# A routed-expert decoder layer on one core: a reworked routing stretch, reordered first transfers, an attention bias added on VectorE, earlier expert loads, and filler matmuls

## The reference, cut to what matters

```python
h = rms_norm(x, norm1_g);  z = h @ w_in            # 11,272 columns
qk = silu(causal_dwconv(concat(qm, km), conv_w))
hm = sigmoid(om) * head_layernorm(mlstm(...));  ha = attention(..., rel_bias)
y = sigmoid(gm) * (hm @ w_branch_m) + sigmoid(ga) * (ha @ w_branch_a)
x = x + y @ w_out
t = rms_norm(x, norm2_g)
pg = softmax(t @ w_grp + b_grp);  el = t @ w_exp + b_exp      # 4 groups, 32 experts
# best group, its best two experts, weights pg * pe / sum(pe)
x = x + sum_e combine[:, e] * ((silu(t @ w1[e]) * (t @ w3[e])) @ w2[e])
out = rms_norm(x, final_g)
```

## Time and profile before

| what | value |
|---|---|
| median of 3 runs | 1272.96 us (1272.76 to 1274.13) |
| the profiled execution: its own time, its span | 1268.82 us, 1267.3 us |
| TensorE matmul busy, weight load busy | 1183.3 us (93%), 886.9 us (70%) |
| DVE, ACT, POOL busy | 689.1 us, 413.2 us, 44.9 us |
| mean granted TensorE clock | 0.986 of full speed |
| expert weight loads | 96 into `w_a` and 96 into `w_b`, 1024 KB each |
| DMA, 40 slices | 130 to 250 GB/s up to the output projection, 425 GB/s in nearly all slices of the experts |

### The profile page before, as it was taken

The page is one execution under the profiler, slowest core; times in us unless marked ns, Lnnn a source line. Parts: engine busy times, 40 slices in busy tenths (PEclk is TensorE's granted clock), DMA queues, the critical chain, the costliest instruction groups (busy, mean ns, idle before and its releaser), DMA issues.

```text
span 1267.3 us, 19180 instructions
## 1 busy us (share of the span) xinstructions
PE 1183.3 (93%) x7194; PEld 886.9 (70%) x7194; DVE 689.1 (54%) x980; ACT 413.2 (33%) x463; POOL 44.9 (4%) x57
## 2 busy tenths in 40 slices
PE   5999999999999999999999985899999999899995
PEld 4888888888888888888888875555554544444442
DVE  4678555554666657567875547243444433433335
ACT  4444333334334354443344443111111211111113
POOL 1000000001002022000000002000000000000000
PEclk9999999999999999999999987999999999999998
DMA  7765565655555455555765635899999999999993
GB/s 245 226 190 175 166 193 172 195 174 178 185 165 167 134 164 165 165 166 182 251 177 181 236 148 226 342 402 425 426 426 425 425 425 425 425 425 424 425 425 150
DMA packets 170146, 336.52 MB, mean 266 GB/s; under 512 B 12144, under 2 KB 136192, under 8 KB 153088
## 3 DMA queue, kind: packets, MB, share of 16 engines
q1 hardware_dynamic: 163088, 335.58, 71.8%
q10 hardware_dynamic: 7024, 0.48, 0.4%
HBM read 333.93 MB, written 2.11 MB: 265 GB/s over the span
## 4 chain that ended last, share of the span: by engine, by line
PE 56%; issue 39%; ACT 1%; DVE 1%; ACTq 1%; POOL 1%; POOLq 0%; DVEq 0%
PE ps L824 19%; PE ps L840 11%; PE ps L826 10%; PE ps L842 6%; PE ps L973 5%; PE ps L974 2%; PE ps L813 1%; POOL h2lo L552 1%; PE ps L942 0%; PE ps L993 0%; ACTq L564 0%; DVE wsplit L1149 0%; ACT xsq L572 0%; ACT h2n L744 0%; ACT wsplit L581 0%
## 5 line engine op out<-in xcount | busy, mean ns | idle before, releaser
L1149 DVE TENSOR_TENSOR wsplit<-wraw,wsplit 128x2048 fp32r<-128x2048 f32 x120 | 277.1, 2309 | 180.5 <-ACT wsplit L581 179.7
L824 PE MATMUL ps<-act_split,wsplit 128*128 128x512 f32 x1024 | 360.7, 397 | 0.0
L581 ACT ACTIVATE wsplit<-wraw 128x2048 fp32r<-128x2048 f32 x120 | 230.0, 1917 | 386.7 <-PE ps L826 204.7
L826 PE MATMUL ps<-act_split,wsplit 128*128 128x256 f32 x1024 | 286.6, 280 | 0.0
L840 PE MATMUL ps<-wsplit,act_split 128*128 128x512 f32 x640 | 226.8, 398 | 2.1 <-DVE wsplit L1149 2.1
L824 PEld LDWEIGHTS ps<-act_split,wsplit 128*128 128x128 f32 x1024 | 192.0, 188 | 46.1 <-DVE wsplit L1149 1.3
L826 PEld LDWEIGHTS ps<-act_split,wsplit 128*128 128x128 f32 x1024 | 193.3, 189 | 0.2
L842 PE MATMUL ps<-wsplit,act_split 128*128 128x256 f32 x640 | 179.2, 280 | 0.0
L840 PEld LDWEIGHTS ps<-wsplit,act_split 128*128 128x128 f32 x640 | 120.1, 188 | 31.3 <-issue 2.7
L1056 PE MATMUL ps<-w_a,xe 128*64 128x256 f32 x1024 | 115.4, 381 | 13.8 <-DMA w_a<-in_w_dram 12.0
L1595 DVE TENSOR_TENSOR hid<-sg,ps 128x128 f32<-128x128 f32 x32 | 9.2, 288 | 206.0 <-ACT sg L769 206.0
(11 more groups left out here) (274 smaller groups left out, 1082.0 us busy)
## 6 DMA issues: line engine op xcount, KB each, us to landing
w_a<-in_w_dram SPq DMA_DIRECT2D x96, 1024.0 KB, 19.0
w_b<-in_w_dram SPq DMA_DIRECT2D x96, 1024.0 KB, 21.3
wraw<-in_w_in_dram SPq DMA_DIRECT2D x88, 1024.0 KB, 5.1
wraw<-in_w_out_dram SPq DMA_DIRECT2D x16, 1024.0 KB, 5.1
wraw<-in_w_branch_m_dram SPq DMA_DIRECT2D x8, 1024.0 KB, 5.1
wraw<-in_w_branch_a_dram SPq DMA_DIRECT2D x8, 1024.0 KB, 5.1
xin<-in_x_dram SPq DMA_DIRECT2D x2, 1024.0 KB, 6.5
x<-in_x_dram SPq DMA_DIRECT2D x1, 2048.0 KB, 9.3
```

What stands on the lines that cost most here:

```text
L581: act.activation(wsplit[:, q % 2, :, 0], wraw[:, q % RAW], ACT.Copy).then_inc(rounded, 1)
L824: pe.matmul(banks[b], w[:, k, 0, b * P:(b + 1) * P], a, start=first and k == 0, stop=False)
L826: last = pe.matmul(banks[b][:, 0:T], w[:, k, 1, b * P:(b + 1) * P], a[:, 0], start=False, stop=last_half and k == HALF_K - 1)
L1149: dve.tensor_tensor(wsplit[:, q % 2, :, 1], wraw[:, q % RAW], wsplit[:, q % 2, :, 0].bitcast(F32), ALU.subtract).then_inc(split, 1)
```

## The change

- *Start.* SP no longer waits between x and the first four weight loads. Five of the nine parameter DMAs move from ACT's queue to SP's, behind these four loads, with a semaphore of their own (`late_loaded`). POOL makes the identity first (`ident_ready`); TensorE runs 12 filler matmuls of it and then transposes the four early parameter rows. DVE squares the second token tile. The product of `relb` and `onehot_s`, the split of `wif` and the trip of the bias through DRAM come after the first units.
- *Bias.* `flip` and its matmuls are gone; DVE adds the bias to the logits (read and written with reversed columns) into `prob`, and ACT takes the exponential from there.
- *Output projection.* ACT also rounds x2 (without the norm) to `x2hi`, DVE subtracts (`x2lo`) unit by unit. The router sums accumulate in two PSUM regions over all units. The last unit is multiplied in three passes of 256 columns in place of 512 and 256, so that no sum of halves is needed, and DVE squares it.
- *Routing.* The norm is left out of the gather; an extra gather of `rms_rep` gives `slot_rms`, by which DVE multiplies when it makes `xe`. The second mask `mk[:, :, 1]` becomes a running sum along the experts (`tensor_tensor_scan`). TensorE runs 20 filler matmuls after the router sums and 12 after the rank sums. POOL no longer works on `h2lo`.
- *Loads.* The hidden weights of expert 1, `w2_b0` and `w2_b1` are loaded as each ring slot comes free in the last halves; `w2_a1` waits for `x2lo_ready`, and `w2_a0` for the gather.

```diff
 sync:
             for t in range(TT):
                 sp.dma_start(xin[:, t], x_v[:, t]).then_inc(x_loaded[t], 16)
-            sp.wait_ge(par_loaded, 16 * 9)
...
             pair(COL_QK, None)
+            sp.dma_start(wif_raw[:], ...).then_inc(late_loaded, 16)
+            sp.dma_start(ifb[:], if_bias.partition_broadcast(P)).then_inc(late_loaded, 16)
+            sp.dma_start(relb[:], rel_bias).then_inc(late_loaded, 16)
+            sp.dma_start(onehot_s[:], onehot).then_inc(late_loaded, 16)
+            sp.dma_start(g2T[:], ...).then_inc(late_loaded, 16)
+            pairs(1, UNITS_QK, COL_QK, 0)
             sp.wait_ge(rev_ready, 1)
             sp.dma_start(rev_dram, rev[:]).then_inc(rev_stored, 16)
             sp.wait_ge(rev_stored, 16)
...
-            pairs(1, UNITS_QK, COL_QK, 0)
...
             for kh in range(2):
                 load_hidden(0, 0, kh)
+            for kh in range(2):
+                sp.wait_ge(split, HALVES + 2 * kh - 2)
+                load_hidden(1, 1, kh)
+            sp.wait_ge(used, HALVES - 1)
+            load_rows(0, lambda b: b, (1,))
             sp.wait_ge(used, HALVES)
-            for kh in range(2):
-                load_hidden(1, 1, kh)
-            load_rows(0, lambda b: b)
+            load_rows(1, lambda b: b + 2, (1,))
             sp.wait_ge(routed, 1)
+            sp.wait_ge(x2lo_ready, UNITS_OUT)
             load_rows(1, lambda b: b + 2, (0,))
-            sp.wait_ge(xg_summed, DC)
-            load_rows(1, lambda b: b + 2, (1,))
+            sp.wait_ge(xg_summed, DC + 1)
+            load_rows(0, lambda b: b, (0,))
 gpsimd:
-            for t, cols in ((0, slice(0, D)), (1, slice(0, D // 2))):
-                pool.wait_ge(h2hi_ready, t + 1)
-                pool.tensor_tensor(h2lo[:, t, cols], h2n[:, t, cols], h2hi[:, t, cols].bitcast(F32),
-                                   ALU.subtract).then_inc(h2lo_ready, 1)
 tensor:
+            for n in range(WARM):                                   # 12
+                pe.matmul(ps[:, 6, 0:P], ident[:], ident[:], start=True, stop=True)
...
-                    pe.matmul(bank[:, 0:P], flip[:], bias[:, 0, P:T], start=False, stop=True)
...
-                    pe.matmul(bank[:, P:REV], flip[:], bias[:, 0], start=False, stop=True).then_inc(logits, 1)
...
+            def token_half_in_place(banks, q, first, last_half):
...
+                        pe.matmul(banks[t][:, 0:UNIT], hi, w[:, k, 0], start=first and k == 0, stop=False)
+                        pe.matmul(banks[t][:, 0:UNIT], hi, w[:, k, 1], start=False, stop=False)
+                        last = pe.matmul(banks[t][:, 0:UNIT], lo, w[:, k, 0], start=False, ...)
...
+            out_pair(UNITS_OUT // 2 - 1, end=True)
+            route(UNITS_OUT // 2 - 1, 0)
             turn_x2(1, UNITS_OUT - 1)
+            route(UNITS_OUT // 2 - 1, 1).then_inc(routed, 1)
+            for n in range(WARM_ROUTE):                             # 20
+                pe.matmul(ps[:, 6, 0:P], ident[:], ident[:], start=True, stop=True)
...
+            for n in range(WARM_SELECT):                            # 12
+                pe.matmul(ps[:, 6, 0:P], ident[:], ident[:], start=True, stop=True)
...
+                    if c is None:
+                        last = pe.matmul(ps[:, n % 8], rms_rep[:, t], sel[:, t].bitcast(F32), ...)
 vector:
+            steps.done(dve.scalar_tensor_tensor(xsq[:, 1], xin[:, 1], 1.0, xin[:, 1], ALU.mult, ALU.mult,
+                                                accum_out=stat[:, 1:2]))
...
+                    dve.tensor_tensor(prob[:, a, P - 1::-1], ps[:, 4 + a, P - 1::-1], bias[:, 0:P], ALU.add)
+                    steps.done(dve.tensor_tensor(prob[:, a, REV - 1:P - 1:-1], ps[:, 4 + a, REV - 1:P - 1:-1],
+                                                 bias[:, 0:T], ALU.add))
...
+            def x2_split(n, u, start):
+                dve.wait_ge(x2hi_ready, n + 1)
+                cols = ds(start, UNIT)
+                dve.tensor_tensor(x2lo[:, :, cols], x2u[:, u], x2hi[:, :, cols].bitcast(F32),
+                                  ALU.subtract).then_inc(x2lo_ready, 1)
...
-            unit_sums = ...
-            for u in range(2):
-                last = dve.tensor_reduce(unit_sums[:, u]..., ps[:, 2 + u, ...]..., AX.X, ALU.add)
+            for t in range(TT):
+                last = dve.scalar_tensor_tensor(lr[:, t], ps[:, 2 + t, 0:n_r], stat[:, 22 + t:23 + t], brt[:],
+                                                ALU.mult, ALU.add)
...
-            dve.tensor_tensor(rt[:, 3], iota_t, by_token(FIRST, EXPERTS), ALU.is_gt)
...
-            steps.done(dve.tensor_tensor(rt[:, 1], iota_t, by_token(FIRST, EXPERTS), ALU.is_gt))
-            dve.tensor_tensor(mk[:, :, 1], rt[:, 3], rt[:, 1], ALU.add).then_inc(mk_ready, 1)
+            x2_split(UNITS_OUT - 1, 1, D - UNIT)
+            for t in range(TT):
+                dve.tensor_scalar(rms_rep[:, t], ones[:], stat[:, 22 + t:23 + t], None, ALU.mult)
...
-                    dve.tensor_copy(xe[:, b], xg[:, :, ds(at, SLOTS)]).then_inc(xe_ready, 1)
+                    factors = slot_rms[:, ds(at, SLOTS)].unsqueeze(1).to_broadcast([P, DC, SLOTS])
+                    dve.tensor_tensor(xe[:, b], xg[:, :, ds(at, SLOTS)], factors, ALU.mult).then_inc(xe_ready, 1)
```

More of the change, by code:

```diff
@@ L623, in _ @@
             conv_pair(0)
+            act.wait_ge(late_loaded, 16 * 5)
+            act.activation(wif[:, :, 0], wif_raw[:], ACT.Copy).then_inc(wif_hi, 1)
             with act.Fori(1, UNITS_QK // 2 - 1) as i:
@@ L724, in out_unit @@
                 act.wait_ge(x2_ready, n + 2)
-                act.activation(x2[:, :, ds(i * (2 * UNIT) + u * UNIT, UNIT)], x2u[:, u], ACT.Copy)
+                if end and u == 1:
+                    x2T_copy(u, n)
+                act.activation(x2[:, :, cols], x2u[:, u], ACT.Copy)
+                act.activation(x2hi[:, :, cols], x2u[:, u], ACT.Copy).then_inc(x2hi_ready, 1)
+                if end and u == 1:
+                    return
                 if not first_unit(i, u):
@@ L865, in _ @@
                 half(channel_half, q, q, None)
+            pe.wait_ge(consts, 1)
+            pe.wait_ge(late_loaded, 16 * 5)
+            pe.matmul(ps[0:A_HEADS, 6, 0:T], relb[:], onehot_s[:], start=True, stop=True).then_inc(rev_summed, 1)
             stage(channel_half, 0, 1, UNITS_QK)
@@ L1032, in _ @@
             last.then_inc(rank_summed, 1)
+            for n in range(WARM_SELECT):
+                pe.matmul(ps[:, 6, 0:P], ident[:], ident[:], start=True, stop=True)
             pe.wait_ge(sel_ready, 1)
[L1036 to L1044 removed]
+            pe.wait_ge(x2lo_ready, UNITS_OUT)
@@ new lines, in _ @@
+            parts = [part[:].rearrange("p t (q c) -> p t c q", c=DC) for part in (x2hi, x2lo)]
+            for n, c in enumerate(gathers):
+                if n >= 8:
+                    pe.wait_ge((xg_act, xg_dve)[n % 2], (n - 8) // 2 + 1)
+                for t in range(TT):
+                    if c is None:
+                        last = pe.matmul(ps[:, n % 8], rms_rep[:, t], sel[:, t].bitcast(F32), start=t == 0, stop=t == TT - 1)
+                        continue
+                    for k, part in enumerate(parts):
+                        last = pe.matmul(ps[:, n % 8], part[:, t, c], sel[:, t], start=t == 0 and k == 0,
+                                         stop=t == TT - 1 and k == 1)
@@ L1302, in _ @@
             dve.wait_ge(o_ready, 1)
-            with steps.loop(0, M_HEADS, 9) as i:
+            dve.wait_ge(flip_loaded, 16 * A_HEADS)
+            with steps.loop(0, M_HEADS, 11) as i:
                 def ahead(q):
```

217 lines of the change are left out of this document (111 added, 106 removed).

## The result

The changed kernel takes 1257.51 us, the median of four runs (1255.45 to 1259.09). The kernel before, in four runs beside it, takes 1272.86 (1268.77 to 1274.13). The ratio is 0.9881, with a 95% interval of 0.986 to 0.9902: faster by 15.3 us. I had forecast 1255.5 within 1250.5 to 1261.5.

What follows compares the result with a forecast made beforehand. TensorE's passes bound the dense stages, the weight stream the experts. Terms -4.6 + 0.4 - 5.3 - 8.0 = -17.5 from the profiled 1268.8 gave 1251.3, plus 4.1 to the median: 1255.5 us, range 1250.5 to 1261.5.

Steps and rivals of the forecast that it cites:

- The bound: From the first expert's upper half on, the weight stream sets the time; using that half earlier moves the end equally.
- Start: Launch to first dense pass: 4.6 us less, with bounds of 5.5 and 3.
- DVE squares tile 2 when it lands: At the start, DVE's square was to run from 8.3 to 9.1 for some 2.4 us, with L813 at 12.5.
- lower bound (3): At the start, only 3 us gained if the weight loads right behind x hold the parameters up.
- Relative bias: In the dense stages, the `relb` product moves into TensorE's full time, two passes of 256 columns: +0.4 us.
- Bias: In the dense stages, TensorE saves 0.66 us for each of 8 heads: -5.3 us; DVE's additions fit its idle time.
- Last halves: Output projection, three passes of 256 columns instead of 512 and 256: taken as 0, bounds 0 and +3.3 us.
- Routing: From the last dense pass to the first expert: -8.0 us in sum.
- POOL's collision: In routing, DVE's two-SBUF-input instructions L1521 and L1486 are slowed beside POOL's L552; without POOL's work -6.0 us.
- a clock of 1.00 through both fillers: Expected sign in the changed profile: TensorE at full clock during the 20 and the 12 routing fillers.
- rival 1: Routing fillers at half clock stand in the way: +4 us at the first gap, +1 at the second, 1260 to 1262; chance 0.12.
- the other reading: Unbroken routing fillers lift the clock themselves, so not all 40 passes are slow: price 1 to 2 us rather than 4.

Runs made afterwards that it cites:

- a_sq_first: The changed kernel with DVE's square of the second token tile put ahead of the parameter copy: 1256.93 us, 0.9881 of before.
- b_lo_on_dve: The kernel before with POOL's part of `h2lo` moved to DVE, behind the mask: 1269.08 us, 0.9978 of before.
- b_dve_bias: The kernel before with the bias alone changed, added by DVE without flipped-identity matmuls: 1266.54 us, 0.9962 of before.
- b_copy: The kernel before, unchanged, profiled again: 1273.59 us, 1.0012 of before.

## Why the prediction was right, and where its terms were off

**The bound.** From the load that the first expert releases to the end, 470.15 us before and 470.33 after. What comes earlier there is gained in full, and the later pairs hide DVE's multiply of `xe`. In the eleven other traces it is 469.3 to 471.0. What the earlier expert loads are worth no run shows alone; the forecast gave them nothing, and the sum leaves nothing for them.

**Start: -3.4, not -4.6.** The step that failed is "DVE squares tile 2 when it lands". It waited for the parameters, at 9.08. My lower bound (3) named the weight loads holding up the parameters; the size is nearly that, but no run shows that the loads are what held them up. a_sq_first puts 0.9 us on the order of DVE's program: there the square starts at 8.69, when x lands, and L819 at 12.65, near my 12.5. "I give them nothing" of the start's fillers was wrong too: without them the first dense pass is 0.6 to 1.7 us later. And I took the diagonal product's 8.6 us as fixed: it took 8.78 to 9.61 us in four executions of the same start, 10.16 without fillers, and 7.31 and 7.38 with ten more.

**Relative bias: +2.0, not +0.4.** The product costs 0.7 where I had 0.4; the other 1.3 are the slower pace of the halves behind it, which other executions of before have too (b_lo_on_dve), so it may be chance and not the change. The trip through DRAM is hidden, as forecast: TensorE's only wait over 0.7 us in 22 to 750 is the 2.1 us behind DVE's `wsplit`, which before has as well.

**Bias: -5.3, confirmed** by the four iterations and by b_dve_bias within its interval. The stretch shows -1.9 only because the two half-clock stretches, +3.2, fell into this execution.

**Last halves: near nothing.** From their first pass to the transposes the last two take 12.48 us instead of 12.19, 0.3 of the bound of 3.3.

**Routing: -6.8, not -8.0.** POOL's collision is as large as forecast. From DVE's resumption to the mask it is 8.0 us less (forecast 7.8). Two sizes are off. DVE goes on 5.6 us behind the last half, not 4.8, because the second router product runs at half clock: 0.8. I had taken 1.20 for both products, though the earlier trace rows have 1.92 for the second. The sign "a clock of 1.00 through both fillers" failed with it (0.58 and 0.56 in 750 to 758). And the fillers end 1.4 us behind the mask, at half clock for their first part: rival 1, in a mild form. I had given that rival 4 us, and put 1 to 2 us behind the other reading, which is what came. Against it, from the rank products to the gather it took 4.57 us at full clock, where before took 5.07, and the gather and the first `xe` +0.9 against 1.1. What the running sum and the fillers behind it share of these 0.5 us, no run separates.

**The squares beside POOL.** The Trainium skill (SBUF — State Buffer, Who interferes with whom) says that a POOL instruction that only writes doesn't disturb DVE's with two SBUF inputs. The trace agrees: L1527 takes 0.43 and 0.42 us, both times beside an iota.

**The median.** I added 4.1 us, the distance of the profiled execution from the median, and it came out 2.0 us too low. Two things in the traces can make up such a distance: stretches at half clock of 1.6 us each (b_copy), and the slower pace, 1.7 us up to `wif` (b_lo_on_dve). By terms, without the two stretches, the span would be 13.1 us shorter than before against 17.5 forecast: 1.2 of the 4.4 missing are the start, 1.6 the relative bias and the pace, 0.3 the last halves, 1.2 the routing, 0.2 the tail. So the mechanisms held, but that the total missed by no more than 2.0 us is in part luck: the terms are 4.4 us too large, and the medians differ by 2.2 us more than the terms, most likely because the execution of before that I built on was a fast one.

**What stays open:** what brings about a stretch at half clock in one execution and not in another (near 299 to 308 in six of the thirteen traces, near 658 to 669 in four), and what sets the pace of 5.55 or 5.65 us. Kernels with the same code up to there have either, so the edits alone don't decide it. The start as a whole, the order of the expert loads and the norm left out of the gather were not run alone; their terms are read from the stretches of the trace.

## What to carry to other kernels

Before you count an instruction as early, read what stands ahead of it in its engine's own program, since a copy that waits for small parameters holds it as surely as a semaphore. Fillers pay when they lead TensorE at full clock into dense work, but what outlasts the wait that they cover is lost: reckon their length at the clock that the gap shows, half of full here, and look at more than one execution, since the same fillers left the clock at 1.00 in three traces and at 0.50 in a fourth. And when a profiled execution lies off the median of its runs by more than the terms you argue about, profile the same kernel again before you explain a difference of that size.

## What the runs showed of the hardware

- A DVE instruction on 2 columns takes 4.10 us beside POOL's two-input pass over SBUF, ending 0.02 us behind it (766.18 and 766.16), and 0.16 when that work is gone (b_lo_on_dve).
- A full dense stage can fall to half clock for some ten passes soon behind a few passes with 4 rows of weights (303 to 307) or a wait of 2.1 us (657.5 to 662); each time costs 1.6 us. Other executions with the same passes and the same wait stay at 1.00.
- The same stage of 16 halves runs at one of two paces, 5.55 or 5.65 us a half, at a granted clock of 1.00 in both, also with unchanged code (88.83 us in before, 90.54 in b_lo_on_dve).
- 64 small passes of the diagonal product took 10.16 us without filler products ahead of them, 8.78 to 9.61 in four executions with 12 (at half clock for a first part), and 7.31 and 7.38 with 22.
